# At the four hand-overs between stages, the split of the normalised input goes through a full-precision buffer

## The reference, cut to what matters

```python
h = _rmsnorm(x, norm_pre[i, 1])          # x * rsqrt(mean(x*x)+eps) * g
a = _memory_cross_attention(h, ...)      # first thing in it: h @ w_q
x = x + _rmsnorm(a, norm_post[i, 1])
```

## Time and the profile before

| | |
|---|---|
| Median of 3 executions | 2869.25 us (2868.25 to 2871.21) |
| The profiled execution | 2871.7 us, of which the span is 2870.1 us |
| PE busy | 2773.4 us, 97% |
| DVE, ACT, POOL busy | 1631.2 us, 1334.9 us, 145.2 us |
| TensorE's clock, mean | 0.976 of full |

### The profile page before, as it was taken

How to read it: one execution, slowest core, us unless ns; L and a number is a source line. 1 busy time by engine, 2 the same in 40 slices (tenths; PEclk the granted TensorE clock), 3 DMA queues, 4 the chain that set the end, 5 groups by cost and what they waited for, 6 DMA issues and landing times. The chain is left out here.

```text
span 2870.1 us, 35813 instructions
## 1 busy us (share of the span) xinstructions
PE 2773.4 (97%) x13081; PEld 2305.7 (80%) x13081; DVE 1631.2 (57%) x1931; ACT 1334.9 (47%) x1571; POOL 145.2 (5%) x115
## 2 busy tenths in 40 slices
PE   7999999989989999999999989999999999999998
PEld 6888888878867888888788868877778888887886
DVE  4577777765465555555544555455455555555444
ACT  4445555444455544544444444342355444454443
POOL 1121111120000000000000000000000000000000
PEclk9899999999989999999999999997999999999999
DMA  6555555536543555555555556640545555555552
GB/s 211 175 167 181 179 190 190 186 137 248 190 147 131 192 182 184 189 181 186 190 190 191 175 189 191 196 157 1 176 161 188 178 189 185 182 188 188 192 190 102
DMA packets 222832, 505.43 MB, mean 176 GB/s; under 512 B 15234, under 2 KB 51122, under 8 KB 202026
## 3 DMA queue, kind: packets, MB, share of 16 engines
q1 hardware_dynamic: 218778, 479.98, 49.7%
q0 software_dynamic: 3984, 24.50, 2.4%
HBM read 499.12 MB, written 5.32 MB: 176 GB/s over the span
## 5 line engine op out<-in xcount | busy, mean ns | idle before, releaser
L1456 DVE TENSOR_TENSOR w_lo<-raw,w_hi 128x2048 fp32r<-128x2048 f32 (+3 forms) x472 | 1036.3, 2201 | 986.9 <-ACT w_hi L644 978.5
L644 ACT ACTIVATE w_hi<-raw 128x2048 fp32r<-128x2048 f32 (+3 forms) x472 | 868.7, 1845 | 1189.6 <-PE PB L1020 783.2
L1018 PE MATMUL PB<-w_hi,hT_hi 128*128 128x512 f32 (+2 forms) x2656 | 1024.4, 386 | 30.3 <-DVE hT_lo L1485 15.5
L1020 PE MATMUL PB<-w_hi,hT_lo 128*128 128x512 f32 (+2 forms) x2656 | 1010.7, 381 | 0.0
L1019 PE MATMUL PB<-w_lo,hT_hi 128*128 128x512 f32 (+2 forms) x2656 | 1010.7, 381 | 0.0
L1018 PEld LDWEIGHTS PB<-w_hi,hT_hi 128*128 128x128 f32 x2656 | 508.1, 191 | 127.6 <-DVE hT_lo L1485 20.6
L1020 PEld LDWEIGHTS PB<-w_hi,hT_lo 128*128 128x128 f32 x2656 | 507.8, 191 | 93.3
L1019 PEld LDWEIGHTS PB<-w_lo,hT_hi 128*128 128x128 f32 x2656 | 508.0, 191 | 90.0 <-issue 1.7
L1064 PE MATMUL PB<-w_hi,hT_hi 128*128 128x512 f32 x560 | 157.4, 394 | 5.7 <-issue 2.4
L1064 PE MATMUL T<-w_hi,hT_hi 128*128 128x512 f32 x560 | 155.8, 391 | 1.3 <-ACT big L776 1.3
L1064 PE MATMUL PB<-w_lo,hT_hi 128*128 128x512 f32 x560 | 156.0, 392 | 0.0
(11 more groups left out here) (253 smaller groups left out, 1630.8 us busy)
## 6 DMA issues: line engine op xcount, KB each, us to landing
raw<-in_ffn_w_up_dram SPq DMA_DIRECT2D x88, 1024.0 KB, 5.0
raw<-in_w_up_dram SPq DMA_DIRECT2D x88, 1024.0 KB, 5.0
raw<-in_ssd_w_in_dram SPq DMA_DIRECT2D x64, 1024.0 KB, 5.3
raw<-in_ffn_w_down_dram SPq DMA_DIRECT2D x44, 1024.0 KB, 4.8
raw<-in_w_down_dram SPq DMA_DIRECT2D x44, 1024.0 KB, 4.9
raw<-in_w_in_dram SPq DMA_DIRECT2D x40, 1024.0 KB, 5.0
raw<-in_ssd_w_out_dram SPq DMA_DIRECT2D x32, 1024.0 KB, 4.8
raw<-in_ssd_w_in_dram SPq DMA_DIRECT2D x64, 256.0 KB, 3.2
```

The lines of the kernel that those rows point to most:

```text
L644: nc.scalar.activation(dst, src, ACT.Copy).then_inc(hi_ready, 1)
L1018: nc.tensor.matmul(o, h, wh[:, c, :], start=(j == first and c == 0), stop=False)
L1020: ins = nc.tensor.matmul(o, l, wh[:, c, :], start=False, stop=(j == last and c == 3))
L1456: V.tensor_tensor(dst, src, h.bitcast(F32), ALU.subtract).then_inc(lo_ready, 1)
```

## The change

It touches the split at the four boundaries and the squares' scratch.

- **ACT.** The four scaled 128x128 blocks of a bank go in fp32 to one of four slots of 128x512 in SBUF. ACT then waits for its own four results (`h_made`) and writes `hT_hi` for the whole bank by one copy from the slot. For tile 1 it first waits until DVE has read the slot's former contents.
- **DVE.** One subtraction of 128x512, slot minus `hT_hi`, both in SBUF, in the place of four scaled subtractions of 128x128 that read PSUM. It frees the PSUM bank as before.
- **Squares.** Their discarded output goes to the second half of the scratch for both tiles, since the slots lie in the first; before the squares of a tile ACT waits for those of the tile before.

```diff
+        def h_slot(n, tt, b):
+            area = tmp_big if n == N_2 else xn_big
+            order = [(0, i) for i in FIRST_TILE_ORDER] + [(1, i) for i in range(4)]
+            k = order.index((tt, b))
+            s = k % 4
+            return area[:, 0, s * BLK:(s + 1) * BLK], order[k - 4] if k >= 4 else None
...
+                    at, again = h_slot(n, tt, b)
+                    if again is not None:
+                        _, _, empty, used = h_bank(n, *again)
+                        act.wait_ge(empty, used + 1)
                     for c in range(4):
-                        k = 4 * b + c
-                        ins = nc.scalar.activation(hT_hi[:, k, tt * P:(tt + 1) * P], bank[:, c * P:(c + 1) * P], ACT.Copy,
-                                                   scale=col(gain, k0 + k))
-                    ins.then_inc(h_hi_done, 1)
+                        ins = nc.scalar.activation(at[:, c * P:(c + 1) * P], bank[:, c * P:(c + 1) * P], ACT.Copy,
+                                                   scale=col(gain, k0 + 4 * b + c))
+                    ins.then_inc(h_made, 1)
+                    act.wait_ge(h_made, split_count(n, tt, b) + 8 * (BY_TILE.index(n) - t_idx(n)))
+                    nc.scalar.activation(hT_hi[:, 4 * b:4 * b + 4, tt * P:(tt + 1) * P],
+                                         at.rearrange("p (c t) -> p c t", t=P), ACT.Copy).then_inc(h_hi_done, 1)
...
             def square_bank(n, tt, nb, src, scratch):
-                ins = nc.scalar.activation(scratch[:, tt, nb * BLK:(nb + 1) * BLK], src, ACT.Square, accum_out=ssq_parts[:, k:k + 1])
+                if n != N_FIN or tt:
+                    act.wait_ge(sq_done, sq_count(n, tt) - 1)
+                ins = nc.scalar.activation(scratch[:, 1, nb * BLK:(nb + 1) * BLK], src, ACT.Square, accum_out=ssq_parts[:, k:k + 1])
...
+                    if n in BY_TILE:
+                        k, s = 4 * b, slice(tt * P, (tt + 1) * P)
+                        V.tensor_tensor(hT_lo[:, k:k + 4, s], h_slot(n, tt, b)[0].rearrange("p (c t) -> p c t", t=P),
+                                        hT_hi[:, k:k + 4, s].bitcast(F32), ALU.subtract).then_inc(empty, 1)
+                        continue
```

More of the change, by code:

```diff
@@ L334, in program @@
         bank_done = sem("bank_done")
-        h_hi_done = sem("h_hi_done")
+        h_hi_done, h_made = sem("h_hi_done"), sem("h_made")
         kT_copied, kv_stored, kv_loaded = sem("kT_copied"), sem("kv_stored"), sem("kv_loaded")
@@ L673, in h_hi @@
                     act.wait_ge(full, uses + 1)
-                    for c in range(4):
-                        k = 4 * b + c
-                        ins = nc.scalar.activation(hT_hi[:, k, tt * P:(tt + 1) * P], bank[:, c * P:(c + 1) * P], ACT.Copy,
-                                                   scale=col(gain, k0 + k))
-                    ins.then_inc(h_hi_done, 1)
+                    if n not in BY_TILE:
+                        for c in range(4):
+                            k = 4 * b + c
+                            ins = nc.scalar.activation(hT_hi[:, k, tt * P:(tt + 1) * P], bank[:, c * P:(c + 1) * P], ACT.Copy,
+                                                       scale=col(gain, k0 + k))
+                        ins.then_inc(h_hi_done, 1)
+                        continue
[3 more added lines that the diff above has]
+                        act.wait_ge(empty, used + 1)
+                    for c in range(4):
+                        ins = nc.scalar.activation(at[:, c * P:(c + 1) * P], bank[:, c * P:(c + 1) * P], ACT.Copy,
[4 more added lines that the diff above has]
+                                         at.rearrange("p (c t) -> p c t", t=P), ACT.Copy).then_inc(h_hi_done, 1)
             def down_first(name, ready):
```

## The result

The changed kernel took 2881.79 us (median of 6 executions, 2881.09 to 2883.81), the kernel before, run beside it, 2869.7 (2868.25 to 2872.15). The ratio is 1.0043, its 95% interval 1.003 to 1.0056: slower, by 12 us where the prediction said 7.9.

A forecast was written before the change was run, and what follows sets the result against it. PE, busy 97% of the span, was taken to wait on ACT's chain at the four boundaries. 3 x 1.91 + 2.13 = 7.9 us on the median of 2869.25, clock net nothing, gave 2877.1 us, range 2870.0 to 2882.0.

The forecast's parts named there:

- What bounds the kernel: All boundaries: PE busy 97% of the span; once the transposes are through, each microsecond added to ACT is added to PE.
- Prices: One bank: ACT's copy 0.62 us plus 0.03 wait, DVE wins 0.43 on the result; squares' wait 0.18 a boundary.
- Step by step: Delays followed through N_H2 and carried to the others: 1.91 us each at N_H1, N_H2, N_1 and 2.13 at N_2.
- the sum: Four boundaries together: 3 x 1.91 + 2.13 = 7.9 us slower.
- The clock: TensorE's clock in tile 1: a fall is worth 1.59 us; idle times near 2.1, so no net change expected.
- The prediction's own sign of being wrong: A copy under 0.45 us, or a clock row in tile 1 staying at 1.00 where it was 0.68.
- ACT's addition is cheap or hidden: Rival, boundaries: DVE's saving reaches PE, 9.0 us faster together, 2860.2; chance of faster 0.08.
- The clock pays it back: Rival, tile 1 at three boundaries: clock stays up, 7.9 - 4.8 = 3.1 us, 2872.4; chance 0.25, shared with low-end copy.
- A dearer hand-over: Rival: N_2 loses its clock too, 2878.7, or wait 0.13 and copy 0.67, 11.3 us, 2880.5; chance 0.17.

The follow-up runs named there:

- The order with the weights first: Two quads of the next unit's weights ahead of the squares at N_H2, N_1, N_2: in the kernel before 2857.59 us, in the changed kernel 2855.37, both 0.9947.
- four roundings: Changed kernel with four ACT copies of 128x128 in the place of one of 128x512 per bank: 2892.87 us, 1.0077 of the kernel before.
- The two repeats: Changed kernel run unchanged twice more, each against the kernel before: 2881.36 us (1.0035) and 2880.87 us (1.003).

## Why the prediction was right or wrong

**What bounds the kernel: right.** ACT's chain behind tile 1's transposes ends at the next unit's weights, and what ACT got more there PE waited more. The order with the weights first shows this from both sides: it takes 15 us from the kernel before, and of the 7.2 us by which the change lengthens PE's idle time it leaves 3.2.

**Prices: right.** The copy was put at 0.62 and is 0.632; the wait for ACT's own result 0.03 and 0.03; the square's wait 0.18 and 0.19; DVE's subtraction 0.68 to 0.69 and 0.690. Not foreseen was that the copy's overlap with what follows is shorter than that of the scaled blocks (0.10 for 0.16), which is the 0.12 between 1.60 and 1.48 on the way to the next unit.

**Step by step: right in the places and close in the sizes.** Quad 3 went from 0.22 to between 0.43 and 0.48 (0.46 forecast), the next unit from 2.66 to between 4.18 and 4.21 (4.1), the evacuation from 5.09 to 6.60 (6.6). The wait of tile 1 had been put at 2.1 at three boundaries: it stayed at 2.17 and 2.18 at N_H2 and N_1 and fell from 2.18 to 1.99 at N_H1. At N_2 it grew from 1.96 to 2.18 (2.15). Compared at full clock in tile 1, ACT's hi of the next unit at N_H2 starts 28.6 us after the start of the products where it was 26.5, 2.1 later (1.9 forecast), and at N_2 28.5 for 26.2, 2.3 later (2.13). The boundaries grew by 7.8 us over three traces of each; the sum was 7.9.

**The clock: the step that failed.** "So I expect no net change" put this term of the sum at nothing. It was argued from the waits of tile 1 alone, as if the lengthened waits for the next unit cost their length and nothing else. The prediction's own sign of being wrong came true: at N_H2 the changed kernel's clock row in tile 1 is 1.00 where it had been 0.68. What the runs showed in its place is two shifts that nearly cancel. Tile 1 lost 12.7 slow products on the mean, 2.5 us: at N_H2 (8, 6, 0 to none) and N_1 (8 to none) though the wait stayed at 2.17 to 2.18, and 2.3 on the mean at N_H1; why the same wait is followed by slow products or not, nothing here explains. The next units got 11 more, 2.2 us, behind waits that are 1.3 to 1.6 us longer. Net that is 0.3 us in the traces, so "no net change" was right in its number by luck and wrong in what it rested on. And where a longer wait was made (four roundings) or taken away (weights first), the slow products went with it, 5.1 us on 5.5 and 3.5 on 12.6.

**The size of the miss.** The change measures 8.6 to 12.3 us, mean 10.3, where the sum has 7.9, while the spans of the three traces of each kernel differ by 8.3. Of the first measurement, 2881.79 - 2877.1 = 4.7 us, 0.45 is the base (2869.7 for 2869.25), 0.4 is what the traces show above the sum, 2.0 is what the timings (10.3) show above the traces, and the other 1.8 is what this measurement shows above the mean of the three. The two repeats' intervals hold 7.9 us, 1.0028; the first one's, from 1.003, does not. Where the 2 us between traces and timings lie stays open. One figure on record points at the clock: the mean granted clock of the repeats and of the executions timed beside them is 0.9770 before (80 executions) and 0.9753 for the changed kernel (18, with the first six), a gap of 0.0016, where the three traces of each, read to four digits, have 0.9764 and 0.9759, a gap of 0.0005. That the traced executions of the changed kernel lost less clock than the others fits, but a low clock costs nothing while PE stands idle, so it is not a proof.

**The rivals.** *ACT's addition is cheap or hidden* is refuted: the waits for `hT_lo`, for `w_lo` and for the evacuation all grew in sum, and DVE waits 40.6 us for the copy. *The clock pays it back* was right for tile 1 at the three boundaries, where 15 slow products fewer are 3.0 us of the 4.8 it counted on, though at two of them the gap was no shorter; 0.5 of it was given back in tile 1 at N_2 and 2.2 at the next units. *A dearer hand-over* is refuted in its price (0.03 and 0.63); its other half, N_2 losing its clock in tile 1, happened in one trace of three. The first measurement lies above its upper number, 2880.5, all the same; the copy and the wait were not dearer, and what was stays open, as said above.

The page Perfetto Trace Analysis in the Trainium skill (Optimizing Scalar/DVE Operations) says that larger operations can help a saturated engine, and smaller pieces one that isn't saturated and leaves gaps on others. ACT was busy for 1355.1 us of 2879.5, 47%, and the grouped form lost about 10 us, which is the outcome that the prediction took from the page. But that doesn't test the rule: for ACT the form is an added copy, not a grouping of what it did. With the roundings in four pieces and one signal the kernel was slower still, and no run here shows smaller pieces helping.

## What to carry to other kernels

Cost an addition to an engine off the bound by what the bound engine waits for next on it, however far behind the edit that is; here three quarters of PE's added idle time fell at weights, and at an evacuation, that stand behind eight squares, and moving the weights ahead of squares whose result is needed later won one and a half times what the change had cost. Expect that a wait of TensorE can cost more than its length: here 12.6 us of waits were worth 15 to 16, and 5.5 more cost 10, though the change's own 7.2 came to 7.8 in the traces. Before putting a term at nothing, look at every wait that the change lengthens, not only at those next to it. For an effect of 0.3%, cut several traces of each kernel at the same instructions before believing one pair.

## What the runs showed of the hardware

The same wait of 2.17 to 2.18 us ahead of the same products was followed by a granted clock of 1.00 or by 6 to 8 products at half clock, and that by execution: at N_H2 6 or 8 slow products in 2 of 3 traces before, 8 of them at N_1 in 3 of 3 before and none in 3 after, 7 at N_2 in 1 of 3 after. In the rows shown the first product after a wait of 4.18 to 8.74 us takes 0.79 to 0.80 us but once (0.51), after 1.96 to 2.87 us 0.50, but once 0.62. An activation that waits for the one before it on the same engine costs its 0.03 us gap plus the lost overlap of 0.10 (behind a 128x512 copy) to 0.16 us (behind a scaled 128x128 block).
